# State-space layers of a four-layer decoder step: the samples' C stationary in column groups, the states moving, the states loaded two slots ahead

## What is computed

```python
    a_cum = jnp.cumsum(adt, axis=-1)
    cb = jnp.einsum('bcign,bcjgn->bcgij', c, b)
    w = cb[:, :, :, None] * jnp.exp(segsum(adt))
    y_diag = jnp.einsum('bcgrij,bcjgrp->bcigrp', w, xdt)
    ...
    y_off = jnp.einsum('bcign,bcgrpn,bcgri->bcigrp', c, new_states[:, :-1], jnp.exp(a_cum))
    y = (y_diag + y_off).reshape(bt, L, H, P)
```

## Time and profile before

| | us |
|---|---|
| median of 3 runs | 2106.91 (2106.85 to 2110.78) |
| profiled execution | 2107.75 |
| its span | 2106.1 |
| TensorE matmul busy | 1934.6 (92%) |
| VectorE busy | 1186.1 (56%) |
| ScalarE busy | 960.5 (46%) |
| GpSimdE busy | 478.6 (23%) |
| mean granted TensorE clock | 0.953 |

### The profile page before, as it was taken

How to read it: one execution, slowest core, us unless ns; L and a number is a source line. 1 busy time by engine, 2 the same in 40 slices (tenths; PEclk the granted TensorE clock), 3 DMA queues, 4 the chain that set the end, 5 groups by cost and what they waited for, 6 DMA issues and landing times. The chain is left out here.

```text
span 2106.1 us, 37643 instructions
## 1 busy us (share of the span) xinstructions
PE 1934.6 (92%) x14726; PEld 1830.9 (87%) x14726; DVE 1186.1 (56%) x2046; ACT 960.5 (46%) x1566; POOL 478.6 (23%) x480
## 2 busy tenths in 40 slices
PE   6899979999998678999997887999998999799999
PEld 4899969999997457999996666999988999699998
DVE  4677764555443235554445775555466777555543
ACT  3666663444342124443343554444347666434432
POOL 3222212333100002442102321333112222023420
PEclk9999989999998688999999998999999999899999
DMA  6367755555552094655656742665563667456554
GB/s 181 98 203 235 235 173 161 160 163 147 172 170 79 17 275 122 169 161 144 176 192 206 288 170 76 176 169 152 164 191 113 221 218 222 135 154 166 161 150 133
DMA packets 502033, 352.63 MB, mean 167 GB/s; under 512 B 14154, under 2 KB 487100, under 8 KB 501084
## 3 DMA queue, kind: packets, MB, share of 16 engines
q1 hardware_dynamic: 495156, 306.03, 49.9%
q0 software_dynamic: 6272, 43.92, 5.5%
q10 hardware_dynamic: 430, 0.29, 0.1%
HBM read 326.58 MB, written 50.63 MB: 179 GB/s over the span
## 5 line engine op out<-in xcount | busy, mean ns | idle before, releaser
L268 PE MATMUL ps<-xh,whi 128*128 128x288 f32 x2368 | 657.8, 304 | 10.0 <-PEq L176 9.9
L268 PE MATMUL ps<-xl,whi 128*128 128x288 f32 x2368 | 647.1, 300 | 0.0
L240 DVE TENSOR_TENSOR wlo<-raw,whi 128x2048 fp32r<-128x2048 f32 (+3 forms) x241 | 501.8, 2083 | 245.2 <-ACT whi L229 245.0
L229 ACT ACTIVATE whi<-raw 128x2048 fp32r<-128x2048 f32 (+3 forms) x241 | 419.1, 1740 | 263.5 <-PE ps L276 231.4
L268 PEld LDWEIGHTS ps<-xh,whi 128*128 128x128 f32 x2368 | 454.7, 192 | 12.2 <-issue 10.5
L268 PEld LDWEIGHTS ps<-xl,whi 128*128 128x128 f32 x2368 | 455.4, 192 | 0.8
L276 PE MATMUL ps<-xh,wlo 128*128 128x288 f32 x2368 | 354.6, 300 | 0.0
L276 PEld LDWEIGHTS ps<-xh,wlo 128*128 128x128 f32 x2368 | 328.8, 190 | 1.1
L520 POOL TENSOR_TENSOR gh<-sg,ut 128x288 f32<-128x288 f32 x88 | 216.3, 2458 | 353.0 <-ACT sg L461 353.0
L268 PE MATMUL ps<-hh,whi 128*128 128x288 f32 x704 | 189.7, 296 | 0.0
L268 PE MATMUL ps<-hl,whi 128*128 128x288 f32 x704 | 189.6, 297 | 0.0
(11 more groups left out here) (319 smaller groups left out, 2702.4 us busy)
## 6 DMA issues: line engine op xcount, KB each, us to landing
raw<-in_ffn_w_in SPq DMA_DIRECT2D x176, 512.0 KB, 5.0
raw<-in_ssm_w_in SPq DMA_DIRECT2D x80, 512.0 KB, 4.8
raw<-in_ffn_w_out SPq DMA_DIRECT2D x64, 384.0 KB, 4.0
raw<-in_ffn_w_out SPq DMA_DIRECT2D x64, 320.0 KB, 3.2
H<-in_state_ssm SPq DMA_DIRECT2D x32, 512.0 KB, 7.6
out_ssm_sample<-H SPq DMA_DIRECT2D x32, 512.0 KB, 6.5
raw<-in_ssm_w_out SPq DMA_DIRECT2D x32, 512.0 KB, 5.0
Kp_L<-in_cache_diff_k SPq DMA_DIRECT2D x64, 256.0 KB, 4.5
```

Of the source, the lines that this page charges most:

```text
L229: act.activation(wts["hi"][:, s, 0:width], raw[:, s, 0:width], ACT.Copy).then_inc(hi_ready.sem, 1)
L240: dve.tensor_tensor(wts["lo"][:, s, 0:width], raw[:, s, 0:width], wts["hi"][:, s, 0:width].bitcast(F32), ALU.subtract).then_inc(lo_ready.s ...
L268: pe.matmul(out, W[0][:, kk, j, :], x_[:, k, :], stop=False, start=(part == 0 and kk == 0 and x_ is seg.hi), skip_group_check=True)
```

## The change

`y_state` is turned round. A tile `Cz` (128 x 4 groups x 8 samples x 32) holds each sample's four columns of C, all else in its 32 columns zero. For each sample `Cz[:, g, b, :]` is stationary (32 columns) and the turned state `HT[:, b, :]` moves (128 columns). The eight samples go to three column groups of 32, at output partitions 32, 64 and 96, and add up there in bank 5. ScalarE copies the three groups (`move_ys`, two copies a chunk) into rows 32 to 127 of `XU[:, c % 2, 5, :]`, the operand of the samples' part of `y_inside`. There the rows of `E` below 32 now hold the decay of each token (the constant `C_TRIS` gets a pattern below row 32, and `cb` is filled with 1 in place of 0), so that `y_inside` adds this part by itself. `take` handles 128 columns in place of 160. `y_state(k-1)` stands ahead of `sums_of_chunk(k-1)` and `turn_x(k)` in place of behind them. GpSimdE fills and spreads `Cz` once (`spread_c`). SyncE loads the state of chunk `k + 2` in place of `k + 1`, after the store of the final states. Some small tiles move into unused columns of `G` and into `sq`.

```diff
-                    if 4 <= k + 1 < CI:
-                        sp.wait_ge(h_out[(k + 1) % 4].sem, h_out[(k + 1) % 4].at((k + 1) // 4))
-                        load_state(k + 1)
                     if k >= 3 and k % 2:
                         store_final(k // 2 - 1)
+                    if 4 <= k + 2 < CI:
+                        sp.wait_ge(h_out[(k + 2) % 4].sem, h_out[(k + 2) % 4].at((k + 2) // 4))
+                        load_state(k + 2)
...
@@ turn_state
                         pe.wait_ge(fs_moved.sem, fs_moved.at(c))
+                        pe.wait_ge(ys_moved.sem, ys_moved.at(2 * c))
...
-                def y_state(c, half):
+                def y_state(c):
                     pe.wait_ge(h_moved.sem, h_moved.at(2 * c + 2))
-                    pe.wait_ge(off_scaled.sem, off_scaled.at(c))
-                    pe.wait_ge(y_taken.sem, y_taken.at(c))
                     if c == 0:
-                        pe.wait_ge(cb_ready.sem, cb_ready.at(2 * GROUPS))
-                    for b in range(4 * half, 4 * half + 4):
-                        at = TOK + P + b * T
-                        mm = pe.matmul(ps[:, 7, at:at + T], HT[:, b, :],
-                                       BC[:, GROUPS + c // 4, SEQ + b * T:SEQ + (b + 1) * T],
-                                       start=True, stop=True, skip_group_check=True)
+                        pe.wait_ge(padded.sem, padded.at(6))
+                    for b in range(NB):
+                        o = 32 * (1 + b % 3)
+                        mm = pe.matmul(ps[o:o + NS, 5, 2 * P:3 * P], Cz[:, c // 4, b, :], HT[:, b, :], start=(b < 3),
+                                       stop=(b + 3 >= NB), tile_position=(0, o), skip_group_check=True)
                     mm.then_inc(ys_mm.sem, ys_mm.inc())
 
                 def y_inside(c):
                     pe.wait_ge(w_ready.sem, w_ready.at(2 * c + 2))
+                    pe.wait_ge(ys_moved.sem, ys_moved.at(2 * c + 2))
...
                     more(L)
+                    y_state(k - 1)
                     sums_of_chunk(k - 1)
                     more(L)
                     turn_x(k)
-                    more(L)
-                    y_state(k - 1, 0)
-                    more(L)
-                    y_state(k - 1, 1)
-                    more(L)
+                    more(L, 3)
                     spread(2 * k)
...
+                y_state(CI - 1)
                 sums_of_chunk(CI - 1)
-                y_state(CI - 1, 0)
-                y_state(CI - 1, 1)
...
+                pool.memset(Cz[:, :, :, :], 0.0).then_inc(padded.sem, padded.inc())
+
+                def spread_c():
+
+                    pool.wait_ge(padded.sem, padded.at(5))
+                    pool.wait_ge(conv_ready.sem, conv_ready.at(EARLY + 1))
+                    own = Cz.rearrange("p g b n -> p g (b n)")
+                    for g in range(GROUPS):
+                        ins = pool.tensor_copy(
+                            bass.AP(own.tensor, own[:, g, 0:1].offset, [own.ap[0], [NS + T, NB], [1, T]]),
+                            BC[:, GROUPS + g, SEQ:TOK].rearrange("p (b t) -> p b t", t=T))
+                    ins.then_inc(padded.sem, padded.inc())
...
+                def move_ys(c):
+                    act.wait_ge(ys_mm.sem, ys_mm.at(c + 1))
+                    if c == 0:
+                        act.wait_ge(padded.sem, padded.at(5))
+                    if c >= 2:
+                        act.wait_ge(y_mm.sem, y_mm.at(2 * c - 2))
+                    for lo, hi in ((NS, 64), (64, P)):
+                        act.activation(XU[lo:hi, c % 2, 5, :], ps[lo:hi, 5, 2 * P:3 * P], ACT.Copy).then_inc(
+                            ys_moved.sem, ys_moved.inc())
...
                         move_s0(k - 1)
                         move_fs(k - 1)
+                        move_ys(k - 1)
...
-                    dve.tensor_tensor(yo[:, :], ps[:, 7, TOK:TOK + P + NS], EA[:, c % 2, :], ALU.mult).then_inc(
+                    dve.tensor_tensor(yo[:, :], ps[:, 7, TOK:TOK + P], EA[:, c % 2, 0:P], ALU.mult).then_inc(
                         off_scaled.sem, off_scaled.inc())
```

More of the change, by code:

```diff
@@ L765, in ssd @@
             BC, xr = sb("BC", [P, 2 * GROUPS, TOK]), sb("xr", [P, 4, TOK])
-            Bt, Bs = sb("Bt", [P, 2, GROUPS * N_STATE]), sb("Bs", [NS, GROUPS * N_STATE])
+            Bt, Cz = sb("Bt", [P, 2, GROUPS * N_STATE]), sb("Cz", [P, GROUPS, NB, NS])
             BtS, Bm = sb("BtS", [3 * NS, GROUPS * N_STATE], F32R), sb("Bm", [P, NB, N_STATE], F32R)
@@ L769, in ssd @@
             XU, dmul = sb("XU", [P, 2, 7, P]), sb("dmul", [P, 7, HEADS])
-            dtk, adk, nack = (sb(n, [P, 3, HEADS]) for n in ("dtk", "adk", "nack"))
-            arg, dec, ea, Dd = sb("arg", [P, 4, HEADS]), sb("dec", [P, 4, HEADS]), sb("ea", [HEADS, 1 + HEADS]), sb("Dd", [HEADS, 2, CI])
+            dtk, adk, arg, dec = (G[:, 8 + n, 96:96 + k * HEADS].rearrange("p (k h) -> p k h", h=HEADS)
+                                  for n, k in enumerate((3, 3, 4, 4)))
+            nack = sb("nack", [P, 3, HEADS])
+            ea, Dd = sb("ea", [HEADS, 1 + HEADS]), sb("Dd", [HEADS, 2, CI])
             acHL, cb = sb("acHL", [P, TOK], F32R), sb("cb", [P, GROUPS, TOK])
@@ L776, in ssd @@
             E, EA = sb("E", [P, 4, TOK]), sb("EA", [P, 2, P + NS])
-            yo, yt, sq = sb("yo", [P, P + NS]), sb("yt", [P, 3, TOK]), sb("sq", [P, 4, TOK])
+            yo, yt, sq = sb("yo", [P, P]), sb("yt", [P, 3, TOK]), sb("sq", [P, 4, TOK])
+            Bs = sq.rearrange("p c n -> p (c n)")[0:NS, 0:GROUPS * N_STATE]
             rs, dsk = sb("rs", [P, 2, TOK]), sb("dsk", [P, CI])
@@ L782, in ssd @@
             strow = H[0:3 * NB, 0:3, :, :].rearrange("p r b n -> p (r b n)")
-            padded = S("rows_padded")
+            padded, ys_moved = S("buffers_filled"), S("probs_scaled")
             tri, tris, same = (cst[:, c:c + P] for c in (C_TRI, C_TRIS, C_SAME))
@@ L1009, in spread @@
                         pe.wait_ge(dec_args.sem, dec_args.at(2))
-                        pe.wait_ge(padded.sem, padded.at(4))
+                        pe.wait_ge(padded.sem, padded.at(5))
                     if h % 2 == 0 and c >= 7:
@@ L1184, in _ @@
                 pool.memset(sp_[:, 0, 64:96], 0.0).then_inc(zeroed.sem, zeroed.inc())
-                pool.memset(cb[:, :, SEQ:TOK], 0.0).then_inc(zeroed.sem, zeroed.inc())
+                pool.memset(cb[:, :, SEQ:TOK], 1.0).then_inc(zeroed.sem, zeroed.inc())
                 pool.memset(XU[:, :, 5, :], 0.0).then_inc(padded.sem, padded.inc())
+                pool.memset(Cz[:, :, :, :], 0.0).then_inc(padded.sem, padded.inc())
[8 more added lines that the diff above has]
+                    ins.then_inc(padded.sem, padded.inc())
                 def conv_ends(n):
@@ L1222, in _ @@
                         conv_ends(n)
+                    if k == 0:
+                        spread_c()
                     weigh(2 * k)
@@ L1324, in move_state @@
                     act.wait_ge(h_turned.sem, h_turned.at(2 * c + half + 1))
-                    act.wait_ge(ys_mm.sem, ys_mm.at(2 * c))
+                    act.wait_ge(ys_mm.sem, ys_mm.at(c))
                     act.activation(HT[:, 4 * half:4 * half + 4, :], ps[:, 5, :], ACT.Copy).then_inc(
@@ L1435, in _ @@
                 move_fs(CI - 1)
+                move_ys(CI - 1)
                 for c in range(4):
@@ L1580, in spread_x @@
                     if c == 0:
-                        dve.wait_ge(padded.sem, padded.at(4))
+                        dve.wait_ge(padded.sem, padded.at(5))
                     dve.wait_ge(x_turned.sem, x_turned.at(c + 1))
@@ L1632, in take @@
                     dve.wait_ge(y_taken.sem, y_taken.at(c + 1))
-                    dve.tensor_tensor(yt[:, r, P:TOK], yt[:, r, P:TOK], yo[:, :], ALU.add).then_inc(
+                    dve.tensor_tensor(yt[:, r, P:2 * P], yt[:, r, P:2 * P], yo[:, :], ALU.add).then_inc(
                         off_added.sem, off_added.inc())
@@ L2905, in shape_constants @@
     c[:NS, C_TRIS:C_TRIS + NS] = same & (s[:, None] <= s[None])
+    c[NS:, C_TRIS:C_TRIS + NS] = i[NS:, None] % NS == i[None, :NS]
     c[:NS, C_SAME:C_SAME + NS] = same
```

## The result

The changed kernel takes 2098.09 us (median of 13 runs, 2087.81 to 2104.51), the kernel before 2108.43 in the same comparison (13 runs, 2105.11 to 2118.15): ratio 0.9933, 95% interval 0.9913 to 0.9954. The forecast was 2111.5. The time lies at the very bottom of the range 2098 to 2121, and on the other side of the kernel before. The profiled execution of the changed kernel took 2102.03 us, with a span of 2100.4; the one of before took 2107.75.

What follows compares the result with a forecast made beforehand. TensorE was taken to bound z slots, a chain over VectorE and ScalarE the x slots. From 2107.75 us, slots 0.0 and clock +4.8 gave 2112.5, less 0.84 for the median, said as 2111.5; range 2098 to 2121.

Steps and rivals of the forecast that it cites:

- the chain's 11.41 us: x slots: time from the start of `spread_x` to TensorE's restart after `HT`, all work of other engines, kept at 11.41 us.
- twelve stalls of 2.0 us: x slots: TensorE idles 2.0 us before `y_state`; seven of twelve such stalls slow the next z slot's clock, +11.2 us.
- TensorE and the chain: z slots are bound by TensorE's queue, x slots by `turn_x`, `spread_x`, VectorE's work and `HT`: -0.73 and +0.88 us each.
- Y = 0.98 in z slots, 0.88 behind a wait: TensorE's time for the new `y_state` in us, in place of 1.71; entering costs about 0.1, covered behind a wait.
- Rival 4: New `y_state`: the column groups don't overlap, so it takes 1.95 us; kernel at 2138 us, chance 0.05.
- rival 5: New `y_state` takes 0.65 us, nearer its lower bound; -10 us before the clock, about 2102 us, chance 0.06.
- Rival 1: TensorE's clock stays up despite the x slots' stalls: -6.4 and 0.0, kernel at 2100.5 us, chance 0.13.
- Slot 15, +1.23: Slot 15: new `y_state` lies ahead of TensorE's wait for ScalarE's root, with two more copies: +0.88 + 0.35 us.
- SyncE: "nothing lost, nothing gained to speak of, as turned states hardly ever waited for a load": State loads two slots ahead, behind the final store: done by about 166 with 3 us left, no gain or loss.
- rival 3: TensorE holds all slots, so each of 32 chunks gains 0.73 us, plus the clock; kernel at 2077 us, chance 0.07.
- rival 2: TensorE's clock falls in every pair of slots, 12 x 1.6 - 6.4 = +12.8 us; kernel at 2119.7, chance 0.25.
- rival 6: SyncE's wait for the store delays the weights; kernel at 2115 to 2125 us, chance 0.02.

Runs made afterwards that it cites:

- experiment 1: Changed kernel with the new `y_state` moved back behind `turn_x` in every slot; 2095.84 us, ratio 0.9944 to the kernel before.
- experiment 3: Kernel before with its old `y_state` moved ahead of `sums_of_chunk` and `turn_x`, nothing else changed; 2148.76 us, ratio 1.0195 to the kernel before.
- experiment 11: Changed kernel with all eight samples' products in one column group in place of three; 2131.09 us, ratio 1.0100 to the kernel before.
- experiment 7: Changed kernel with states loaded one slot ahead, ahead of the weights, in place of two ahead; 2116.66 us, ratio 1.0025 to the kernel before.
- experiment 10: Changed kernel with states loaded one slot ahead and GpSimdE's cache copies cut to one row each; 2093.68 us, ratio 0.9922 to the kernel before.

## Why the prediction was wrong, step by step

The kernel was forecast a little slower and became faster. Two terms failed: the chain's 11.41 us, taken for a constant (it came to 10.97), and, hanging on it, twelve stalls of 2.0 us that were to cost +11.2 us of clock and cost none.

- *TensorE and the chain*: right. z slots are TensorE's, x slots the chain's, and `spread_x` starts 2.08 us after the opening. Experiments 1 and 3 show it from both sides.
- *Y = 0.98 in z slots, 0.88 behind a wait*: the steps of 0.111 us held (0.78 from start to start, 0.1 for the load behind). The 0.1 for entering didn't show up in z slots: they lost 0.82 to 0.92, not 0.73. Rival 4 fell with experiment 11; rival 5, a Y of 0.65, isn't needed.
- *11.41 us "all of it work of other engines"*: this is the term that failed first, by 0.44 us in eight x slots and 0.50 in four, 5.5 us. Its length was taken for a constant, though two of its taps were long only because `weigh` stood beside them. When the chain starts 0.88 later, the meeting falls elsewhere. 13.05 came (12.99 in slots 7 and 11), not 13.48.
- *Twelve stalls of 2.0 us, seven of which cost the clock*: the price, 1.6 us, was measured (13.86 and 12.28), and for stalls of 2.02 and 3.19 us so was the rate, eight of twelve. But eight stalls were 1.35 us, mostly because of the step above, and four were 0.23, as TensorE had waited 1.05 us for ScalarE's root earlier in those slots (the forecast has such a wait in slot 15 alone). Such stalls cost nothing: 0 in place of +11.2. It also didn't help that slot 15 was the model: there 2.95 us of idling stand beside other thin work. Rival 1 (the clock stays up, -6.4) happened, for a reason it hadn't: a gap too short, rather than a gap of 2.0 us too short to count. The new `y_state` itself counts as well, as experiment 3 has the same gap ahead of the old one, and a low clock in ten of twelve z slots. Whether it is the 128 columns or the 0.78 us in place of 1.71 isn't shown. That the low clock of the four old z slots is gone, -6.4, was foreseen, but it is partly luck of the one profile: like kernels had one or two such slots.
- *Slot 15, +1.23*: the root came 1.5 us later against the opening, where 1.23 was foreseen, and 1.2 came back behind it. The stretch of low clock, present in both kernels, lay more under the wait and less over work.
- *SyncE: "nothing lost, nothing gained to speak of, as turned states hardly ever waited for a load"*: the end of this step was right and its reason wrong. The changed kernel has no such wait. But without the early load it would have been some 19 us slower. It was not that the loads had no time to spare: eight of the twelve issued in x slots landed 3.4 us or more ahead of their use. Their landing time was taken for a constant, as the taps' was, and it isn't one: with the new `y_state` the load of slot 5 goes out 0.9 us later against the slot's opening and the cache copies 1.0 us earlier, and 8.6 us become 12.8. The four that took 11.4 to 12.4 us in the kernel before, one of them with a wait of 0.34, were the sign.
- *The sum*: loops 0.0 forecast, -9.0 measured without the clock (in the first layer -1.1 against the forecast from z slots, -2.8 from x slots, +0.4, -0.9 and -0.2 from the rest); clock in the loops +4.8 forecast, -6.1 measured in one execution; +9.4 elsewhere, which no term of the forecast covers. The forecast had its own two gains about right and charged too much for both of the losses. Its chances don't add up as said: rivals 1 and 3 alone make the 0.20 for faster, and rivals 2, 4 and 6 make 0.32, so that 0.47 for slower takes in a third of the forecast's own chance, not nearly half. That the time lies inside the range by 0.1 us is luck.

## What to carry to other kernels

When a kernel is balanced, with TensorE's queue, a chain over VectorE and a transfer all about as long as a slot, its rare waits of 0.2 or 0.3 us each name a limit that can take over as soon as the others give way, and each may need its own edit before any of them pays. For a transfer read the landing times, all of them and not their median, beside the time of use. Choose the order slot by slot: the same product belongs ahead of the transposes where TensorE's queue sets the length, and behind them where the chain does and no other queue comes late by it, as ScalarE's root does in slots 7 and 11 (ratio 0.9894 against 0.9933). And don't carry over a duration along a chain, or a landing time, whose start you move without asking what will stand beside it on the other engines and queues.

## What the runs showed of the hardware

- A VectorE operation with both inputs in SBUF grows beside a GpSimdE product: a gate from 0.46 us to 1.06, and six taps from 2.81 to 3.73 us beside two products; state updates that read PSUM don't.
- TensorE's granted clock stayed at 1.00 after gaps of 1.35 and 1.71 us ahead of 128-column matmuls in three column groups (16 of 16). It fell to 0.50 beside four of four gaps of 2.02 us there and four of eight of 3.19; waits of 2.02 and 2.37 us for loads, elsewhere in a slot, left it at 1.00. Behind gaps of 0.8 to 1.35 us ahead of four-column matmuls it fell in ten of twelve z slots; with gaps of 0.2 at most, in the kernel before, in four of twelve.
- 16 matmul records of 128 columns take 0.78 us to the next instruction's start in three column groups of 32, and 1.86 in one.
- A 512 KB load issued just ahead of GpSimdE's cache copies took 11.2 to 13.6 us in eleven of twelve cases (experiment 7), and 6.5 to 9.0 with the copies cut to a few rows (experiment 10); the one issued at 156.08 in the changed kernel, behind the weights and the store, took 4.1.
